# The experts' up pieces beside the selection: two halves of u in one matmul, added by GpSimd

## Chip, cores, metric

The kernel runs on one core of a Trainium2 chip. The metric is the device time of one execution in microseconds (us).

## What is computed

Two transformer blocks over 256 tokens of width 1024. The change lies in the second block's expert layer (PEER), whose core in the reference is

```python
s1 = jnp.einsum('thd,hnd->thn', qh[..., :PEER_HALF], sub_keys[:, 0])
s2 = jnp.einsum('thd,hnd->thn', qh[..., PEER_HALF:], sub_keys[:, 1])
v1, i1 = lax.top_k(s1, PEER_TOPK)
v2, i2 = lax.top_k(s2, PEER_TOPK)
cand = v1[..., :, None] + v2[..., None, :]          # per head 16 x 16
vs, ci = lax.top_k(cand, PEER_TOPK)
idx = e1 * PEER_KEYS + e2                           # from i1, i2 and ci
g = jax.nn.softmax(vs, axis=-1)
z = jnp.einsum('td,thkd->thk', xc, u_experts[idx])
a = jax.nn.gelu(z) * g
return jnp.einsum('thk,thkd->td', a, v_experts[idx])
```

There are 128 x 128 experts and 8 heads that select 16 each. The kernel does not gather: it computes z for all experts, applies Gelu, multiplies by a map of weights that is zero for experts not selected, and multiplies by all of v_experts.

## The kernel before, in words

**Numbers.** Every large product is made of float32 operands split in a high part (rounded to fp32r) and a low part (the rest), by three matmuls: high x high, high x low, low x high (`mm3`, lines 197 to 201).

**Pieces.** All weights come as one stream of pieces of 128x1024 float32 (512 KB), in the order in which they are used. A ring of four holds them: SyncE (SP) loads `raw`, ScalarE (ACT) makes `w_hi` by a Copy (line 178), VectorE (DVE) makes `w_lo = raw - w_hi` (line 180), and TensorE (PE) uses both. `next_piece` issues the split of the piece three ahead (`split(c + AHEAD)`), and then lets PE wait for its own. ACT's Copy for piece c waits until PE has used piece c - 4; SP loads a slot again when DVE has split it. The last PE instruction of a piece frees the slot (`s_used`).

**Up pieces.** Piece `tile` of the experts' up stream holds 128 experts (columns) by 1024 features. `piece_b` accumulates 8 steps of k into 256 columns (tokens) of a bank: 24 matmuls of 128x256, with `w_hi` or `w_lo` as the stationary operand and `u_hi[:, k, :]` or `u_lo[:, k, :]` as the moving one. `expert_up(q, tile)` (line 1468) uses bank 4 + q, q alternating, and ACT writes Gelu of it into `Z`. PE may start a tile when the Gelu of the tile two before it is done (`s_z`).

**Selection.** Per head, `select(h)` is a chain of small DVE instructions in 12 steps: a copy of the head's scores, maxima, index searches and replacements (steps 1 to 4, on 128 columns), a cast and the candidates' sums (step 5), the same on 256 columns (steps 6 to 8), comparisons and products of two tensors (steps 9 and 10, four each), two reductions (11 and 12). All of them read and write parts of `Z` that no up tile has reached yet.

**Order of the work.** A loop on PE, ACT and DVE runs 8 iterations, one head and 8 up tiles each. `weave(ups(), select(h), 2)` writes the order out: a tile, two steps of the selection, a tile, and so on, so that tiles 0 to 5 of an iteration are followed by two steps each on DVE and tiles 6 and 7 by none. On ACT a table of functions is loaded again at each iteration's start, once for the Copy and once for Gelu.

After the loop, 4 more tiles (`ups2`) alternate with `weigh`, the softmax of the chosen scores and six transposes of PE. In front of them `scores_read`, a small memset of `rows_a` on DVE, tells ACT that the selection no longer reads the part of `Z` that they overwrite. Then comes the stage of the remaining 60 tiles: DVE makes one-hot rows (line 1603) into `rows_a` and others, ACT weighs them (line 1619), PE multiplies them into maps of weights (line 1630), and ACT and DVE bring the maps and the tiles together (lines 1640 to 1668). Last comes the down stage, 128 pieces with matmuls of 512 columns.

GpSimd (POOL) issues DMAs in the first 785 us and nothing afterwards.

Of the kernel before, what the change touches and what calls it, by code (L numbers as in the profile page):

```python
# [7 lines left out]
F32R = mybir.dt.float32r  # L8
U32 = mybir.dt.uint32
ALU = mybir.AluOpType  # L10
ACT = mybir.ActivationFunctionType
AX = mybir.AxisListType
ENG = mybir.EngineType


P = 128
T, D = 256, 1024
NT, KD = T // P, D // P
# [26 lines left out]
RING = 4  # L45
# [44 lines left out]
def build(nc, stream, x_in, gains1, gains2, gain_cols, conv_w, w_ada, b_ada, c_cols, kept_in, rope_in, na_mask_in,  # L90
          t5_in, t5_hot, rpb_pad, sinks, sub_keys, gain_out, out):
    ctx = ExitStack()
    with ctx:
        def sb(c, name, shape, dt=F32):
            return c.enter_context(nc.sbuf_tensor(name, shape, dt))

        def sem(name):
            return ctx.enter_context(nc.semaphore(name))
# [8 lines left out]
        raw = sb(ctx, "raw", [P, RING, PIECE])  # L107
        w_hi = sb(ctx, "w_hi", [P, RING, PIECE], F32R)
        w_lo = sb(ctx, "w_lo", [P, RING, PIECE], F32R)
        u_hi = sb(ctx, "u_hi", [P, KD, T], F32R)  # L110
        u_lo = sb(ctx, "u_lo", [P, KD, T], F32R)
        a_hi = sb(ctx, "a_hi", [P, 2, T], F32R)
        a_lo = sb(ctx, "a_lo", [P, 2, T], F32R)
        kept = sb(ctx, "kept", [P, 2 * P + PT])
# [30 lines left out]
        s_t5c = sem("s_t5c")  # L145
        s_park, s_back, s_out = sem("s_park"), sem("s_back"), sem("s_out")
        s_z = sem("s_z")
        s_chain = sem("s_chain")
        s_eq = sem("s_eq")
        s_hs = sem("s_hs")  # L150
# [7 lines left out]
        AC = Line(nc.scalar, sem("s_ac"))  # L158
        VE = Line(nc.vector, sem("s_ve"))
        lines = (PE, AC, VE)  # L160
        compute = bass.OrderedEngineSet([ENG.PE, ENG.Activation, ENG.DVE])
        V, S, M, G = nc.vector, nc.scalar, nc.tensor, nc.gpsimd

        at = {"piece": 0, "quads": 0}
# [27 lines left out]
        def used(instruction):  # L192

            instruction.then_inc(s_used, 1)
            return s_used, dyn(RING) + at["piece"]
# [7 lines left out]
        def piece_b(o, rhs_hi, rhs_lo, kt=KD, parts=1, last=False, ready=None):  # L203

            s = next_piece(last)
            for part in range(parts):
                for k in range(kt):
                    if ready is not None:
                        PE.wait(*ready[k])
                    col = (part * kt + k) * P  # L210
                    i = mm3(o[part], w_hi[:, s, col:col + P], w_lo[:, s, col:col + P],
                            rhs_hi[:, k, :], rhs_lo[:, k, :], k == 0, k == kt - 1)
            return used(i)

        def piece_a(o, lhs, ks, width, first, final):
# [25 lines left out]
        def take(i):  # L241
            PE.wait(*free.get(i, ()))
# [227 lines left out]
        def weave(main, side, every=1):  # L470

            for n, _ in enumerate(main):
                for _ in range(every):
                    next(side, None)
            for _ in side:
                pass
# [987 lines left out]
        VE.wait(m)  # L1464
        CH = Line(nc.vector, s_chain)
        S.sem_inc(s_z, 2)

        def expert_up(q, tile):

            nc.tensor.wait_ge(s_z, tile + 1)  # L1470
            m = piece_b([bank[4 + q][:, 0:T]], *U)
            nc.scalar.wait_ge(*m)
            nc.scalar.activation(Z[:, bass.ds(tile * T, T)], bank[4 + q][:, 0:T],  # L1473
                                 ACT.Gelu_apprx_tanh).then_inc(s_z, 1)

        def top16(rows_of, m):

# [15 lines left out]
        def select(h):  # L1493

            m = CH.go((), V.tensor_copy, hs, scores[:, bass.ds(h, 1), :].rearrange("p a n -> p (a n)"))
            for a2 in (0, 2):
                yield from top16([(hs[:, a * PK:(a + 1) * PK], hs2[:, a * PK:(a + 1) * PK],
                                   val[:, a, :], idx[:, a, :].bitcast(U32)) for a in (a2, a2 + 1)], m)
            m = got["chain"]
            m1 = CH.go((m,), V.tensor_copy, idxf.rearrange("p t s n -> p (t s n)"),  # L1500
                       idx.rearrange("p a n -> p (a n)").bitcast(U32))
            v4 = val.rearrange("p (t s) n -> p t s n", s=2)
            for tt in range(NT):
                m = CH.go((m,), V.tensor_tensor,
                          cand[:, tt * 256:(tt + 1) * 256].rearrange("p (i j) -> p i j", j=PT),
                          v4[:, tt, 0, :].unsqueeze(2).to_broadcast([P, PT, PT]),
                          v4[:, tt, 1, :].unsqueeze(1).to_broadcast([P, PT, PT]), ALU.add)
            yield
            yield from top16([(cand[:, tt * 256:(tt + 1) * 256], cand2[:, tt * 256:(tt + 1) * 256],
                               pick[:, 0, tt * PT:(tt + 1) * PT],  # L1510
                               pick[:, 1, tt * PT:(tt + 1) * PT].bitcast(U32)) for tt in range(NT)], m)
            m = got["chain"]
            places = pick[:, 1, :].bitcast(U32)
            CH.go((m,), V.tensor_scalar, pick_hl[:, 0:32].bitcast(U32), places, 4, None,
                  ALU.logical_shift_right)
            m2 = CH.go((m,), V.tensor_scalar, pick_hl[:, 32:64].bitcast(U32), places, 15, None,
                       ALU.bitwise_and)
            CH.go((m,), V.tensor_copy, best[:, :, bass.ds(h * PT, PT)],
                  pick[:, 0, :].rearrange("p (t n) -> p t n", t=NT))
            m = CH.go((m2, m1), V.tensor_copy, pick_f, pick_hl.bitcast(U32))  # L1520
            yield

            e5 = [eq.rearrange("p (t k m) -> p t k m", t=NT, k=PT),
                  cand2.rearrange("p (t k m) -> p t k m", t=NT, k=PT)]
            jobs = [(side, tt) for side in range(2) for tt in range(NT)]
            ms = [CH.go((m,), V.tensor_tensor, e5[side][:, tt],
                        pick_f[:, 32 * side + PT * tt:32 * side + PT * (tt + 1)].unsqueeze(2).to_broadcast(
                            [P, PT, PT]),
                        iota16.unsqueeze(1).to_broadcast([P, PT, PT]), ALU.is_equal)
                  for side, tt in jobs]  # L1530
            yield
            ms = [CH.go((ms[n],), V.tensor_tensor, e5[side][:, tt], e5[side][:, tt],
                        idxf[:, tt, side, :].unsqueeze(1).to_broadcast([P, PT, PT]), ALU.mult)
                  for n, (side, tt) in enumerate(jobs)]
            yield
            for side in range(2):
                CH.go((ms[2 * side + 1],), V.tensor_reduce, rowcol[:, side, :, bass.ds(h * PT, PT)],
                      e5[side], AX.X, ALU.add)
                yield


        quads0, piece0 = at["quads"], at["piece"]
        with nc.Fori(0, PH, engines=compute) as h:
            at["quads"], at["piece"] = quads0 + h * (SEL_PIECES // RING), piece0
            CH.restart()

            def ups():
                for j in range(SEL_PIECES):
                    expert_up(j % 2, h * SEL_PIECES + j)
                    yield  # L1550
            weave(ups(), select(h), 2)
            nc.vector.wait_ge(s_chain, CH.n)
            nc.vector.sem_clear(s_chain)
# [4 lines left out]
        def weigh():  # L1558
            b4 = best.rearrange("p t (h k) -> p (t h) k", k=PT)
            m = VE.go((), V.tensor_tensor, cand[:, 0:NT * P].rearrange("p (g k) -> p g k", k=PT), b4,  # L1560
                      b4[:, :, 0:1].to_broadcast([P, NT * PH, PT]), ALU.subtract)
            m = AC.go((m,), S.activation, best.rearrange("p t n -> p (t n)"), cand[:, 0:NT * P], ACT.Exp)
            yield
            m = VE.go((m,), V.tensor_reduce, smx[:, 0, :], b4, AX.X, ALU.add)
            m = VE.go((m,), V.reciprocal, smx[:, 1, :], smx[:, 0, :])
            m = VE.go((m,), V.tensor_tensor, b4, b4, smx[:, 1, :].unsqueeze(2).to_broadcast(
                [P, NT * PH, PT]), ALU.mult)
            yield
            PE.wait(m)
            for a, src in enumerate((best, rowcol[:, 0, :, :], rowcol[:, 1, :, :])):  # L1570
                for tt in range(NT):
                    i = M.transpose(bank[a][:, tt * P:(tt + 1) * P], src[:, tt, :], ident)
            t = PE.done(i)
            yield
            for a in range(3):
                m = VE.go((t,), V.tensor_copy, sel[:, a, :], bank[a][:, 0:T])
            got["sel"] = m
            yield

        def ups2():  # L1580
            for j in range(RING):
                expert_up(j % 2, n0 + j)
                yield

        scores_read = VE.done(V.memset(rows_a[:, 0, 0, 0:1], 0.0))
        AC.wait(scores_read)
        weave(ups2(), weigh())
        AC.wait(got["sel"])
        VE.wait(got["sel"])
# [78 lines left out]
            V.tensor_tensor(zj, zj, fresh[:, q, cut:T], ALU.mult).then_inc(s_mu, 1)  # L1668

        take(6), take(7)  # L1670
        steps = PK - FIRST
        every = steps // (groups - steps)
        made = mapped = applied = 0
# [241 lines left out]
```

## Time and profile before

| what | value |
|---|---|
| median of 3 runs | 1813.37 us (1812.82 to 1814.57) |
| the profiled execution | 1814.04 us |
| its span | 1812.6 us |
| granted clock of TensorE, mean | 0.984 |
| instructions | 33242 |
| loop of the selection, by the trace | 1017 to 1205 us |
| four tiles and softmax behind it | to 1216 us |
| stage of the maps | to about 1445 us |
| down stage and the end | to 1812 us |

The span is the time from the first to the last instruction of the one profiled execution; the time of an execution is slightly longer. Busy times of engines overlap. A matmul's duration in the rows (0.28 us for 256 columns) is longer than the distance between two, since they are pipelined: the pace is read from starts or counts. The same holds for DVE and ACT to a smaller degree. "idle before" is the engine's idle time in front of the instruction, with what released it.

### The profile page before, as it was taken

The page shows a single profiled execution, that of the slowest core. Times are in us where ns is not written, and L with a number is a line of the kernel's source. Part 1 is how long each engine was busy: PE and PEld are TensorE (multiplying, and loading weights), DVE is VectorE, ACT ScalarE, POOL GpSimd, SP SyncE. Part 2 cuts the span into 40 slices and gives each one's busy share as a digit, 9 for nine tenths or more (in the row PEclk, how much of TensorE's full clock was granted, in tenths as well). Part 3 has the DMA queues.
Part 4 walks back from the last instruction along what each step waited for, and adds up shares of the span by engine and source line. Part 5 has one row for each costly group of instructions (what it writes and reads, how often), then busy time and mean ns, then how long its engine had stood idle before and what let it go on. Part 6 is the DMA issues. An engine that isn't in the chain of part 4 may idle for free.

```text
span 1812.6 us, 33242 instructions
## 1 busy us (share of the span) xinstructions
PE 1729.1 (95%) x11638; PEld 1589.1 (88%) x11638; DVE 1353.1 (75%) x2358; ACT 911.8 (50%) x1601; POOL 63.7 (4%) x116
## 2 busy tenths in 40 slices
PE   7999899999999899978979999999999999999996
PEld 6999799988999788967869999999999988888885
DVE  6986688877976678867665799997888856666665
ACT  3345444444354434444534455567777644554553
POOL 0000011000000112100000000000000000000000
PEclk9999999999999999999989999999999999999998
DMA  6555588754444699853325355554444455555554
GB/s 206 204 187 196 171 319 274 256 186 142 161 150 165 200 340 291 253 159 105 117 70 206 125 174 180 185 186 141 139 134 136 140 174 197 190 191 196 188 194 139
DMA packets 91753, 333.87 MB, mean 184 GB/s; under 512 B 11016, under 2 KB 11192, under 8 KB 91216
## 3 DMA queue, kind: packets, MB, share of 16 engines
q1 hardware_dynamic: 79776, 289.06, 48.2%
q0 software_dynamic: 10912, 39.38, 6.6%
q10 hardware_dynamic: 976, 4.19, 0.6%
q8 instruction: 62, 1.02, 0.2%
q14 instruction: 27, 0.22, 0.0%
HBM read 330.46 MB, written 6.07 MB: 186 GB/s over the span
## 4 chain that ended last, share of the span: by engine, by line
PE 78%; DVE 14%; issue 3%; ACT 3%; DMA 2%; DVEq 0%; SPq 0%; ACTq 0%
PE bank L199 24%; PE bank L200 23%; PE bank L201 23%; DVE Z L84 6%; DVE w_lo L180 4%; PE bank L1630 3%; PE bank L249 1%; DMA raw<-stream 1%; ACT w_hi L178 1%; PE bank L1234 1%; DVE yc L84 1%; PE bank L459 1%; ACT space L84 1%; DVE st L84 1%; PE bank L743 1%
## 5 line engine op out<-in xcount | busy, mean ns | idle before, releaser
L180 DVE TENSOR_TENSOR w_lo<-raw,w_hi 128x1024 fp32r<-128x1024 f32 x546 | 661.4, 1221 | 175.9 <-ACT w_hi L178 174.4
L199 PE MATMUL bank<-u_hi,w_hi 128*128 128x256 f32 x2416 | 703.4, 291 | 23.3 <-DVE w_lo L180 10.8
L178 ACT ACTIVATE w_hi<-raw 128x1024 fp32r<-128x1024 f32 x546 | 573.7, 1052 | 278.8 <-PE bank L201 202.0
L200 PE MATMUL bank<-u_lo,w_hi 128*128 128x256 f32 x2416 | 688.1, 285 | 0.0
L201 PE MATMUL bank<-u_hi,w_lo 128*128 128x256 f32 x2416 | 688.1, 285 | 0.0
L199 PEld LDWEIGHTS bank<-u_hi,w_hi 128*128 128x128 f32 x2416 | 468.3, 194 | 38.1 <-issue 12.4
L200 PEld LDWEIGHTS bank<-u_lo,w_hi 128*128 128x128 f32 x2416 | 468.3, 194 | 4.8 <-issue 2.4
L201 PEld LDWEIGHTS bank<-u_hi,w_lo 128*128 128x128 f32 x2416 | 467.6, 194 | 0.0
L199 PE MATMUL bank<-w_hi,a_hi 128*128 128x512 f32 x768 | 300.2, 391 | 3.7 <-DVE a_lo L937 1.8
L200 PE MATMUL bank<-w_lo,a_hi 128*128 128x512 f32 x768 | 299.6, 390 | 0.0
L201 PE MATMUL bank<-w_hi,a_lo 128*128 128x512 f32 x768 | 298.8, 389 | 0.0
L199 PEld LDWEIGHTS bank<-w_hi,a_hi 128*128 128x128 f32 x768 | 144.4, 188 | 33.1 <-DVE a_lo L937 2.7
L201 PEld LDWEIGHTS bank<-w_hi,a_lo 128*128 128x128 f32 x768 | 144.2, 188 | 30.4
L200 PEld LDWEIGHTS bank<-w_lo,a_hi 128*128 128x128 f32 x768 | 144.4, 188 | 27.7
L1705 ACT ACTIVATE a_hi<-Z 128x256 fp32r (+1 forms) x128 | 53.4, 418 | 174.1 <-PE bank L201 172.3
L1707 DVE TENSOR_TENSOR a_lo<-Z,a_hi 128x256 fp32r<-128x256 f32 x128 | 54.4, 425 | 85.4 <-ACT a_hi L1705 85.4
L1619 ACT ACTIVATE rows_a<-rows_a,sel 128x128 f32<-128x128 f32 x256 | 80.8, 390 | 0.0
L1603 DVE TENSOR_TENSOR rows_a<-kept,sel 128x512 f32<-128x512 f32 x64 | 44.2, 691 | 36.5 <-PE bank L1630 36.4
L926 ACT ACTIVATE qT<-bank 128x256 f32<-128x256 f32 x64 | 24.5, 382 | 85.6 <-PE bank L201 85.5
L1473 ACT ACTIVATE Z<-bank 128x256 f32 (+1 forms) x68 | 26.1, 384 | 78.9 <-PE bank L201 78.8
L961 DVE SCALAR_TENSOR_TENSOR space<-gate,c_tmp,space 128x1024 f32 x48 | 61.4, 1280 | 0.4
L935 DVE CAST a_hi<-qT 128x256 fp32r<-128x256 f32 x64 | 19.2, 300 | 48.8 <-PE bank L201 47.9
(263 smaller groups left out, 1657.2 us busy)
## 6 DMA issues: line engine op xcount, KB each, us to landing
raw<-stream SPq DMA_DIRECT2D x546, 512.0 KB, 3.3
gate<-w_ada POOLq DMA_DIRECT2D x48, 512.0 KB, 6.5
space<-b_ada POOLq DMA_DIRECT2D x6, 512.0 KB, 4.6
t_rows<-t_by_distance POOLq DMA_DIRECT2D x8, 256.0 KB, 4.5
rpb_rows<-rpb_pad POOLq DMA_DIRECT2D x8, 224.0 KB, 4.0
gains<-gains POOLq DMA_DIRECT2D x3, 512.0 KB, 5.3
bias_a<-t_rows POOLq DMA_DIRECT2D x1, 1536.0 KB, 11.0
bias_b<-rpb_rows POOLq DMA_DIRECT2D x16, 96.0 KB, 7.7
```

The lines of the kernel that those rows point to most:

```text
L84: return self.done(method(*args, **kw))
L178: nc.scalar.activation(w_hi[:, s, :], raw[:, s, :], ACT.Copy).then_inc(s_hi, 1)
L180: nc.vector.tensor_tensor(w_lo[:, s, :], raw[:, s, :], w_hi[:, s, :].bitcast(F32), ALU.subtract).then_inc(s_split, 1)
L199: M.matmul(o, lh, rh, start=start, stop=False, skip_group_check=True)
L200: M.matmul(o, lh, rl, start=False, stop=False, skip_group_check=True)
L201: return M.matmul(o, ll, rh, start=False, stop=stop, skip_group_check=True)
L961: nc.vector.scalar_tensor_tensor(total, ada_raw[:, k % ADA_RING, :], c_act[:, k:k + 1], total, ALU.mult, ALU.add).then_inc(s_ada, 1)
L1603: return V.tensor_tensor(out, iota.unsqueeze(1).to_broadcast([P, GROUP, P]), values.unsqueeze(2).to_broadcast([P, GROUP, P]), ALU.is_equal)
L1619: i = S.activation(rows_a[:, q, e, :], rows_a[:, q, e, :], ACT.Copy, scale=share[:, e:e + 1])
L1630: i = M.matmul(bank[6 + q][:, e * P:(e + 1) * P], rows_a[:, q, e, :], rows_b[q][:, e, :].bitcast(F32), start=True, stop=True, skip_group_c ...
L1705: S.activation(a_hi[:, q, :], zj, ACT.Copy).then_inc(s_ah, 1)
L1707: V.tensor_tensor(a_lo[:, q, :], zj, a_hi[:, q, :].bitcast(F32), ALU.subtract).then_inc(s_al, 1)
```

## The change

`u_hi` and `u_lo` become one buffer, `u_both`, in which for each k the 256 columns of the high part lie before the 256 of the low part. A new `piece_halves` multiplies `w_hi` by both in one matmul of 512 columns, which fills a whole bank, and adds `w_lo` times the high part to its first 256 columns: 16 matmuls for 24, over the same number of columns. The wanted sum is then first half plus second half. For the 68 tiles of the loop and of `ups2`, ACT copies the whole bank to SBUF (into `rows_a`, unused at that time), GpSimd adds the two halves into `Z`, and ACT applies Gelu in place, one tile later (`activated`). PE's wait is now for the Copy (`s_late`) of the tile two before, ACT's Copy waits for the add (`s_halves`) of the tile two before. GpSimd joins the loop. `scores_read` is a memset of `fresh` in place of `rows_a`, and GpSimd waits for it too. In front of the stage of the maps DVE waits for the last add and PE for the last Copy. The remaining 60 up tiles keep `piece_b`.

```diff
--- before.py
+++ after.py
@@ -107,8 +107,8 @@
         raw = sb(ctx, "raw", [P, RING, PIECE])
         w_hi = sb(ctx, "w_hi", [P, RING, PIECE], F32R)
         w_lo = sb(ctx, "w_lo", [P, RING, PIECE], F32R)
-        u_hi = sb(ctx, "u_hi", [P, KD, T], F32R)
-        u_lo = sb(ctx, "u_lo", [P, KD, T], F32R)
+        u_both = sb(ctx, "u_both", [P, KD, 2, T], F32R)
+        u_hi, u_lo = u_both[:, :, 0, :], u_both[:, :, 1, :]
         a_hi = sb(ctx, "a_hi", [P, 2, T], F32R)
         a_lo = sb(ctx, "a_lo", [P, 2, T], F32R)
         kept = sb(ctx, "kept", [P, 2 * P + PT])
@@ -145,6 +145,7 @@
         s_t5c = sem("s_t5c")
         s_park, s_back, s_out = sem("s_park"), sem("s_back"), sem("s_out")
         s_z = sem("s_z")
+        s_halves, s_late = sem("s_halves"), sem("s_late")
         s_chain = sem("s_chain")
         s_eq = sem("s_eq")
         s_hs = sem("s_hs")
@@ -158,7 +159,8 @@
         AC = Line(nc.scalar, sem("s_ac"))
         VE = Line(nc.vector, sem("s_ve"))
         lines = (PE, AC, VE)
-        compute = bass.OrderedEngineSet([ENG.PE, ENG.Activation, ENG.DVE])
+        compute_list = [ENG.PE, ENG.Activation, ENG.DVE]
+        compute = bass.OrderedEngineSet(compute_list)
         V, S, M, G = nc.vector, nc.scalar, nc.tensor, nc.gpsimd
         at = {"piece": 0, "quads": 0}
@@ -210,6 +212,17 @@
                     col = (part * kt + k) * P
                     i = mm3(o[part], w_hi[:, s, col:col + P], w_lo[:, s, col:col + P],
                             rhs_hi[:, k, :], rhs_lo[:, k, :], k == 0, k == kt - 1)
+            return used(i)
+        def piece_halves(b):
+            s = next_piece()
+            for k in range(KD):
+                w = slice(k * P, (k + 1) * P)
+                M.matmul(b[:, :], w_hi[:, s, w], u_both[:, k, :, :].rearrange("p a t -> p (a t)"), start=k == 0,
+                         stop=False, skip_group_check=True)
+                i = M.matmul(b[:, 0:T], w_lo[:, s, w], u_hi[:, k, :], start=False, stop=k == KD - 1,
+                             skip_group_check=True)
             return used(i)
         def piece_a(o, lhs, ks, width, first, final):
@@ -1464,14 +1477,28 @@
         VE.wait(m)
         CH = Line(nc.vector, s_chain)
         S.sem_inc(s_z, 2)
-        def expert_up(q, tile):
-            nc.tensor.wait_ge(s_z, tile + 1)
-            m = piece_b([bank[4 + q][:, 0:T]], *U)
+        S.sem_inc(s_late, 2)
+        G.sem_inc(s_halves, 2)
+        def expert_up(q, tile, gelu=None):
+            halves = rows_a[:, q, :, :].rearrange("p a n -> p (a n)")
+            zj = Z[:, bass.ds(tile * T, T)]
+            nc.tensor.wait_ge(s_late, tile + 1)
+            m = piece_halves(bank[4 + q])
             nc.scalar.wait_ge(*m)
-            nc.scalar.activation(Z[:, bass.ds(tile * T, T)], bank[4 + q][:, 0:T],
-                                 ACT.Gelu_apprx_tanh).then_inc(s_z, 1)
+            nc.scalar.wait_ge(s_halves, tile + 1)
+            nc.scalar.activation(halves, bank[4 + q][:, :], ACT.Copy).then_inc(s_late, 1)
+            G.wait_ge(s_late, tile + 3)
+            G.tensor_tensor(zj, halves[:, 0:T], halves[:, T:2 * T], ALU.add).then_inc(s_halves, 1)
+            if gelu is not None:
+                activated(gelu)
+        def activated(tile):
+            zj = Z[:, bass.ds(tile * T, T)]
+            nc.scalar.wait_ge(s_halves, tile + 3)
+            nc.scalar.activation(zj, zj, ACT.Gelu_apprx_tanh).then_inc(s_z, 1)
         def top16(rows_of, m):
@@ -1540,14 +1567,15 @@
         quads0, piece0 = at["quads"], at["piece"]
-        with nc.Fori(0, PH, engines=compute) as h:
+        with nc.Fori(0, PH, engines=bass.OrderedEngineSet([*compute_list, ENG.Pool])) as h:
             at["quads"], at["piece"] = quads0 + h * (SEL_PIECES // RING), piece0
             CH.restart()
             def ups():
                 for j in range(SEL_PIECES):
-                    expert_up(j % 2, h * SEL_PIECES + j)
+                    expert_up(j % 2, h * SEL_PIECES + j, h * SEL_PIECES + j - 1 if j else None)
                     yield
+                activated(h * SEL_PIECES + SEL_PIECES - 1)
             weave(ups(), select(h), 2)
             nc.vector.wait_ge(s_chain, CH.n)
             nc.vector.sem_clear(s_chain)
@@ -1579,11 +1607,13 @@
         def ups2():
             for j in range(RING):
-                expert_up(j % 2, n0 + j)
-                yield
-        scores_read = VE.done(V.memset(rows_a[:, 0, 0, 0:1], 0.0))
+                expert_up(j % 2, n0 + j, n0 + j - 1 if j else None)
+                yield
+            activated(n0 + RING - 1)
+        scores_read = VE.done(V.memset(fresh[:, 0, 0:1], 0.0))
         AC.wait(scores_read)
+        G.wait_ge(*scores_read)
         weave(ups2(), weigh())
         AC.wait(got["sel"])
         VE.wait(got["sel"])
@@ -1668,6 +1698,8 @@
             V.tensor_tensor(zj, zj, fresh[:, q, cut:T], ALU.mult).then_inc(s_mu, 1)
         take(6), take(7)
+        V.wait_ge(s_halves, FIRST + 2)
+        M.wait_ge(s_late, FIRST + 2)
         steps = PK - FIRST
         every = steps // (groups - steps)
         made = mapped = applied = 0
```

## Rows read from the trace of the kernel before

**Rows 1.** The page's part 1, busy time of each engine over the span
```profile
PE 1729.1 (95%) x11638; PEld 1589.1 (88%) x11638; DVE 1353.1 (75%) x2358; ACT 911.8 (50%) x1601; POOL 63.7 (4%) x116
```

**Rows 2.** Busy time by stretch: us, then each engine's busy time (instructions)
```profile
1045.00:1070.00 25.00, 25.00 (x209) 24.82 (x208) 24.86 (x84) 14.66 (x20) 0.00 (x0) 1.00 0.55 175
1070.00:1095.00 25.00, 24.98 (x209) 24.78 (x208) 24.86 (x82) 13.65 (x20) 0.00 (x0) 1.00 0.55 183
...
1215.00:1250.00 35.00, 35.00 (x299) 35.00 (x298) 28.29 (x48) 27.27 (x76) 0.00 (x0) 1.00 0.47 151
1600.00:1700.00 100.00, 100.00 (x443) 82.81 (x442) 60.43 (x75) 50.65 (x74) 0.00 (x0) 1.00 0.58 192
```

**Rows 3.** Waits from 1040 to 1200 us: us in total, times, longest
```profile
ACT Z L1473 <- PE bank L201: 65.3, 48, 1.5
...
PEld bank L199 <- DVE w_lo L180: 1.3, 6, 0.2
DVE w_lo L180 <- ACT w_hi L178: 0.9, 1, 0.9
```

**Rows 4.** Groups of instructions, shapes apart, 1019 to 1217 us
```profile
L180 DVE TENSOR_TENSOR w_lo<-raw,w_hi 128x1024 fp32r<-128x1024 f32 x67 | 80.1, 1213 | 5.6 <-ACT w_hi L178 5.6
L178 ACT ACTIVATE w_hi<-raw 128x1024 fp32r<-128x1024 f32 x68 | 71.6, 1053 | 3.0 <-DVE rows_a L1585 3.0
L1473 ACT ACTIVATE Z<-bank 128x256 f32 x64 | 24.6, 384 | 76.5 <-PE bank L201 76.4
L84 DVE TENSOR_TENSOR Z<-Z 128x256 f32<-128x256 f32 x50 | 19.0, 419 | 0.3
```

**Rows 5.** DVE in order of time: start us, us, what [idle before]
```profile
1021.95 1.23 DVE L180 TENSOR_TENSOR w_lo<-raw,w_hi 128x1024 fp32r<-128x1024 f32 x1 [1.79 <-ACT w_hi L178]
...
1042.31 1.23 DVE L180 TENSOR_TENSOR w_lo<-raw,w_hi 128x1024 fp32r<-128x1024 f32 x1 [0.89 <-ACT w_hi L178]
1043.46 0.42 DVE L84 COPY Z<-Z 128x512 f32 x1
...
1066.79 0.42 DVE L84 COPY Z<-Z 128x512 f32 x1
...
1074.19 0.19 DVE L84 CAST Z<-Z 128x64 f32<-128x64 uint32 x1
...
1077.86 0.41 DVE L84 MATCH_REPLACE8 Z<-Z 128x256 f32<-128x256 f32 x1
...
1081.69 1.42 DVE L84 TENSOR_TENSOR Z<-Z,kept 128x256 f32<-128x256 f32 x4
...
1086.70 3.49 DVE L180 TENSOR_TENSOR w_lo<-raw,w_hi 128x1024 fp32r<-128x1024 f32 x3
```

**Rows 6.** PE in order of time, the start of a tile
```profile
1062.08 0.28 PE L201 MATMUL bank<-u_hi,w_lo 128*128 128x256 f32 x1
1062.33 0.39 PE L199 MATMUL bank<-u_hi,w_hi 128*128 128x256 f32 x1
```

**Rows 7.** ACT in order of time, end of one iteration, start of the next
```profile
1062.49 0.38 ACT L1473 ACTIVATE Z<-bank 128x256 f32 x1 [1.54 <-PE bank L201]
1062.95 1.28 ACT L178 ACT_TABLE_LOAD   x1
```

**Rows 8.** A group of instructions, 900 to 1020 us
```profile
L84 ACT ACTIVATE Z<-bank 128x512 f32<-128x512 f32 x8 | 4.8, 595 | 11.7 <-PE bank L201 11.7
```

**Rows 9.** Groups of instructions of POOL, whole span
```profile
L1060 POOL DMA_DIRECT2D bias_b<-rpb_rows x16 | 10.9, 680 | 1.1 <-issue 0.9
...
L1909 POOL MEMSET const-bfloat16-1.0<- 128x1 bf16 x1 | 0.1, 102 | 0.0
```

**Rows 10.** ACT in order of time, after the loop
```profile
1215.93 0.39 ACT L1473 ACTIVATE Z<-bank 128x256 f32<-128x256 f32 x1 [2.32 <-PE bank L201]
...
1217.16 2.44 ACT L1619 ACTIVATE rows_a<-rows_a,sel 128x128 f32<-128x128 f32 x8
```

**Rows 11.** DVE in order of time, after the loop
```profile
1215.89 0.69 DVE L1603 TENSOR_TENSOR rows_a<-kept,sel 128x512 f32<-128x512 f32 x1
```

## The prediction

> **What bounds the kernel now.** I read the page first: PE is busy for 95% of the span, DVE for 75%, ACT for 50% [rows 1]. These are means over stages, and the change touches one: 68 up tiles of the experts, from 1017 to 1216 us, 64 of them in a loop of 8 iterations that also holds the selection. So I read the stretches next. In the loop the column of PE shows 24.98 of 25 us, but that of DVE shows 24.86 of 25, against 28.29 of 35 in the stage behind it [rows 2]. Two engines are full at once. PE's x209 in 25 us is a matmul every 0.1196 us, so an iteration (8 tiles of 24 matmuls) is 22.96 us of PE. DVE's iteration is read from one instruction that comes once in it, the copy of the scores: 1043.46 and 1066.79, that is 23.33 us [rows 5].
>
> Which of the two sets the pace, the waits say. From 1040 to 1200 us DVE waits once, 0.9 us at the start; PE waits for w_lo six times, 1.3 us in all [rows 3], once an iteration, as at 1062.33, where the tile starts 0.25 us behind the matmul before it and not 0.12 [rows 6]. That is the picture of a DVE that never rests and a PE that catches up with it at the end of each iteration, where two tiles come without selection work and w_lo is made three times in a row [rows 5]. PE's slack is 0.4 us of 23.3. ACT is at 14.66 of 25 us and POOL does nothing at all here [rows 2].
>
> **The change part by part.**
>
> *Matmuls.* Per k three of 256 columns become one of 512 and one of 256. A 256 goes by every 0.1196 us. The down stage has 512 alone: x443 in 100 us, 0.2257 us each [rows 2]. So a k saves 2 x 0.1196 - 0.2257 = 0.0135 us, a tile of 8 saves 0.108, 68 tiles 7.3 us of PE. The streamed columns are the same; only the weight change between the two halves is saved. In the loop PE's iteration becomes 22.1 us beside 23.33 of DVE, and DVE's instructions in it are unchanged. DVE covers it: worth 0 there. PE waits longer for w_lo, 1.2 us an iteration where it was 0.4.
>
> *ACT.* A Gelu of 256 columns out of the bank, 0.384 us [rows 4], becomes a Copy of 512 out of a bank, 0.595 us [rows 8], and a Gelu of 256 in SBUF, taken as 0.38 too. A tile costs ACT 1.05 + 0.60 + 0.38 = 2.0 us of 2.9: it fits. PE is now released by the Copy and not by the Gelu, some tenths sooner, which PE does not need. At an iteration's end ACT must wait for the last tile's add before its Gelu, and only then comes the table load of 1.28 us [rows 7] and the next w_hi; that w_hi comes some 1.5 us later behind its tile than now. The tile itself ends about 1.1 us sooner by PE's gain, and the w_hi is needed only behind two other w_lo, so I take 0. At the start DVE idled 1.79 us because w_hi stood behind the first Gelu's table load [rows 5]; now a Copy of 0.6 stands there: -1.0 us.
>
> *GpSimd.* 68 adds of 128x256 fp32 out of SBUF. No row shows one. Duration: below, DVE's pass of this shape, 0.42 us [rows 4]; above, both operands one after the other and the fixed 0.10 of POOL's smallest instruction, 2 x 0.42 + 0.10 = 0.94 [rows 4, 9]. I take 0.10 + 0.42 = 0.52, in the order of POOL's DMA instructions here [rows 9]. The add itself is hidden: its result is wanted one tile later, 2.8 us. The question is what it does to DVE. If the two engines read SBUF by ways of their own, nothing. If they share one, a DVE instruction that needs it waits for the whole add. DVE uses two ways where it reads two tensors, and plausibly in a copy: the copy moves 512 columns in 0.42 us, a two-tensor pass 256 in 0.42 [rows 4, 5]. Between 0 and a full add each time nothing in this trace decides; I take the shared way, for the two engines have no row together that excludes it, and DVE has no idle time to lose it in.
>
> By the Trainium skill, "SBUF — State Buffer", section "SBUF: two separate sides", VectorE and GpSimd share one read and write pair as an exclusive lock, held for an instruction, and a VectorE instruction with two SBUF inputs waits for a GpSimd one that reads SBUF. It speaks against this change, and no row of this trace can show it. "GPSIMD Engine Reference", section "Performance versus the Vector engine", gives 4497 ns for an add of 2048 columns; an estimate from it is 0.56 us for 256, and the sum below would be 1.0 us larger.
>
> Where the adds fall: the iteration whose tile 0 starts at 1062.33 [rows 6]. With 2.76 us a tile PE ends them at 1065.1, 1067.9, 1070.6, 1073.4, 1076.1, 1078.9, 1081.7, 1084.5 (w_lo of tiles 5, 6 and 7 end at 1074.2, 1077.8 and 1081.7 [rows 5], in time). The Copy puts an add 0.7 us behind each. At 1065.8 DVE is in the threefold w_lo, behind it stands the copy of the scores at 1066.79: the add slips in and the copy waits. 1068.6 and 1071.3 fall among maxima and index searches of one tensor: free. 1074.1 is the end of w_lo, in front of a cast and two sums at 1074.19: a hit. 1076.8 falls in w_lo, the add runs behind it beside MATCH_REPLACE8 at 1077.86: free. 1079.6: free. 1082.4 is within the eight two-tensor passes from 1081.69: a hit. 1085.2: w_lo, then reductions of one tensor: free. Three of eight: 3 x 0.52 x 8 iterations = +12.5 us, on DVE's path, which is the loop's.
>
> *Behind the loop.* In the four tiles there DVE, ACT and PE take turns through the softmax; ACT's extra 0.2 us in that chain and PE's 0.1 a tile cancel: 0. Then the one-hot rows share a buffer with the halves, so DVE waits for the last add and PE for the last Copy. Now the last Gelu starts at 1215.93 and the first one-hot runs at 1215.89, before it [rows 10, 11]. After: the Copy ends 0.7 us behind the tile, and PE, which is full here [rows 2], stands that long; Gelu, add and Gelu push w_hi and the weighing of rows, at 1217.16 now, back by some 1.3 us, of which 0.6 is not covered by PE's own delay: +1.3 us. Queued behind the waits are on DVE four one-hots and a w_lo; w_lo leads by three tiles and is not late.
>
> *Moved to strides:* u_hi and u_lo lie alternately; all writes keep runs of at least 128 columns: 0. Pool's loop has an engine of its own with nothing queued, and SP's loads follow DVE's w_lo as before: 0.
>
> **Sum.** 12.5 - 1.0 + 1.3 = +12.8 us on the profiled execution of 1814.04 us (span 1812.6), 1826.8. The median is 0.7 lower, 1813.37: 1826.
>
> **Rivals.**
> *No shared way.* Then DVE's 23.33 us stay, the loop's gain on PE vanishes into waits for w_lo, the 1.0 at the start is lost again at the first boundary, and the one-hots cost 1.3: 1814.7. For it: ACT and DVE work side by side here at unchanged durations (w_hi 1053 ns [rows 4]). Against it: nothing in the trace. 0.25.
> *PE sets the pace (faster).* If DVE's 23.33 were partly waiting for PE in disguise, all 7.3 us would count: 1813.4 - 7.3 + 1.3 = 1807.4. For it: PE is within 0.4 us of DVE. Against: PE's six waits for w_lo, and no wait of DVE. It decides below 22.1 us of DVE work an iteration, and there are 23.3. 0.10.
> *DVE goes first where both want the way.* Then adds are put off behind runs of two-tensor passes and cost about 0.4 us an iteration: 3 + 1.3 gives 1818. Part of the forecast's case, 0.15.
> *The adds become the bound.* With its waits an add above 2.76 us holds ACT's next Copy and, through it, PE. At 0.5 us more a tile that is 32 us: 1845 and more. Against: 0.94 is my upper bound. 0.05.
> *The forecast,* 0.45: 1822 with 0.42 us an add (10.1 us) to 1843 with 0.94 and a fourth hit (30 us).
>
> **Numbers.** Range 1811 to 1843: it leaves out most of the faster case and the tail of the last, and takes in both bounds of the add. 0.2% (3.6 us) is about what a measurement tells from no change. Slower: 0.45 + 0.14 + 0.05 = 0.64, same: 0.25 and the rest of a gentle lock, 0.26, faster 0.10.
>
> **What would show it.** After: the copy of the scores every 24.9 us; DVE's mean for w_lo and two-tensor passes in the loop up from 1213 and 419 ns, or gaps in front of them, those of one-tensor passes not; PEld waiting for w_lo 2.5 us and more an iteration; POOL x68 of 0.5 to 0.9 us. A period of 23.3 us means no shared way, one of 22.1 that PE was the bound. An add above 2 us, or PE waiting for ACT's Copy within the loop, would make the forecast wrong upward.

## The result, and the profile after

| kernel | median, us | ratio to before, 95% interval | DVE's iteration, us |
|---|---|---|---|
| before | 1813.87 | | 23.33 |
| the change | 1829.72 | 1.0089 (1.0078 to 1.0099) | 25.11 |

The change is slower by 15.9 us. The profiled execution's span is 1828.0 us, 15.4 above that of before.

The page's first part, then two stretches of the loop (the columns of [rows 2]), of the changed kernel:

```profile
PE 1726.9 (94%) x11094; PEld 1557.2 (85%) x11094; DVE 1368.0 (75%) x2358; ACT 947.7 (52%) x1669; POOL 128.5 (7%) x184
```

```profile
1045.00:1070.00 25.00, 22.85 (x129) 19.36 (x128) 24.67 (x73) 17.38 (x27) 7.69 (x8) 1.00 0.53 174
1070.00:1095.00 25.00, 22.86 (x128) 19.30 (x128) 24.68 (x75) 17.28 (x27) 7.54 (x8) 1.00 0.51 160
```

PE's busy time fell from 24.98 of 25 us to 22.86: the change gave it time, and the kernel makes nothing of it. DVE is as full as before (24.68), and POOL, idle before, is busy for 7.5 us. The waits in the loop, 1040 to 1200 us (answering to [rows 3]):

```profile
PEld bank L222 <- DVE w_lo L182: 17.9, 18, 1.6
PE bank L222 <- DVE w_lo L182: 12.8, 12, 1.3
ACT Z L1501 <- POOL Z L1494: 6.2, 6, 1.0
DVE w_lo L182 <- ACT w_hi L180: 1.3, 7, 0.2
```

PE's loads waited six times for w_lo before, 1.3 us; now eighteen times, 17.9 us. DVE still waits for almost nothing. So DVE is the path, as before, and its iteration is longer. DVE in order of time, one iteration of the changed kernel (answering to [rows 5]):

```profile
1042.06 0.96 DVE L84 COPY Z<-Z 128x512 f32 x1
...
1066.03 1.23 DVE L182 TENSOR_TENSOR w_lo<-raw,w_hi 128x1024 fp32r<-128x1024 f32 x1 [0.19 <-ACT w_hi L180]
1067.17 0.97 DVE L84 COPY Z<-Z 128x512 f32 x1
...
1075.23 1.30 DVE L84 TENSOR_TENSOR Z<-Z 128x256 f32<-128x256 f32 x2
...
1083.05 1.97 DVE L84 TENSOR_TENSOR Z<-Z,kept 128x256 f32<-128x256 f32 x4
1084.95 1.42 DVE L84 TENSOR_TENSOR Z<-Z 128x256 f32<-128x256 f32 x4
```

The copy of the scores, the clock of the loop, comes at 1042.06 and at 1067.17: 25.11 us, where it was 23.33. The same rows tell where the 1.78 us are. The copy takes 0.97 us and not 0.42. The two sums of candidates take 1.30 us and not 0.87. The four comparisons take 1.97 us and not 1.42; the four products behind them are at their old 1.42. Together 0.55 + 0.43 + 0.55 = 1.53 us. Each is a hold: one DVE instruction stands for a while, and its row is longer by that. GpSimd's rows show by what:

```profile
1066.73 1.12 POOL L1494 TENSOR_TENSOR Z<-rows_a 128x256 f32 x1 [3.75 <-ACT rows_a L1492]
1069.16 0.74 POOL L1494 TENSOR_TENSOR Z<-rows_a 128x256 f32 x1 [1.31 <-ACT rows_a L1492]
...
1074.62 1.62 POOL L1494 TENSOR_TENSOR Z<-rows_a 128x256 f32 x1 [1.55 <-ACT rows_a L1492]
...
1083.18 0.90 POOL L1494 TENSOR_TENSOR Z<-rows_a 128x256 f32 x1 [2.27 <-ACT rows_a L1492]
```

An add that meets nothing takes 0.74 us. The one of 1066.73 comes while DVE is in w_lo (until 1067.17), waits, and runs under the copy of the scores. That of 1074.62 comes within w_lo as well, takes 1.62 us, and the sums are late. That of 1083.18 gets in among the comparisons. So the hold goes both ways: an add waits for a DVE pass under way, and DVE's next pass of that kind waits for the add. The group means over 1040 to 1200 us tell two kinds apart:

```profile
L182 DVE TENSOR_TENSOR w_lo<-raw,w_hi 128x1024 fp32r<-128x1024 f32 x51 | 62.2, 1228 | 1.3 <-ACT w_hi L180 1.3
L84 DVE TENSOR_TENSOR Z<-Z 128x256 f32<-128x256 f32 x36 | 16.1, 486 | 0.2
...
L84 DVE MAX8 Z<-Z 128x8 f32<-128x128 f32 x56 | 13.5, 283 | 0.2
L84 DVE TENSOR_TENSOR Z<-Z,kept 128x256 f32<-128x256 f32 x24 | 11.8, 552 | 0.0
```

In the same stretch before, the passes of two tensors took 418 and 417 ns; they now average 486 and 552. Maxima, which read one tensor, stand at 283 ns, 282 before.

The rest of the iteration, 0.25 us, is mostly the wait of 0.19 at 1066.03: ACT's w_hi is late. ACT at the end of an iteration:

```profile
1063.10 0.42 ACT L1501 ACTIVATE Z<-Z  x1 [1.01 <-POOL Z L1494]
1063.64 1.28 ACT L180 ACT_TABLE_LOAD   x1
1064.94 1.06 ACT L180 ACTIVATE w_hi<-raw 128x1024 fp32r<-128x1024 f32 x1
```

Gelu of the last tile waits 1.01 us for its add, and the table load and w_hi stand behind it. Three of the six whole iterations behind the first take 25.37 us instead: in them a fourth add holds a w_lo too, 1.47 us for 1.21.

Behind the loop, DVE and then PE of the changed kernel:

```profile
1219.59 0.96 DVE L84 TENSOR_TENSOR Z<-Z 128x256 f32<-128x256 f32 x1
...
1229.58 0.69 DVE L1633 TENSOR_TENSOR rows_a<-kept,sel 128x512 f32<-128x512 f32 x1 [0.47 <-POOL Z L1494]
```

```profile
1229.07 0.36 PE L201 MATMUL bank<-u_both,w_hi 128*128 128x256 f32 x1 [1.04 <-ACT rows_a L1492]
```

The softmax's first pass is held by the first of the four adds there (0.96 us for 0.42), the first one-hot waits 0.47 us for the last add, and PE stands 1.04 us for the last Copy. From the small memset at the end of the selection to a fixed instruction of the maps' stage (ACT into `fresh`, 128x4) it is 19.27 us and was 17.31.

The sum by the two traces, from the first copy of the scores to the memset, to that instruction, and to the end: the loop 202.16 - 188.32 = +13.84 us, behind it +1.96, the down stage +1.7. The stages ahead of the loop ended 2.2 us earlier. These last two are not put down to the change: over all runs here the loop starts between 1013.9 and 1017.9 us, and the last stage takes either 363.1 to 363.2 or 364.7 to 364.8 us, whatever the kernel (the longer in the change, five_of_eight and memset_beside). What sets it is open.

### The profile page after: what moved, and what is told of

It reads as the page before. It is cut to its first block, busy times and chain, and to the rows that moved or that the text cites. A ratio compares the mean times of both kernels' runs of the same rounds, so it can differ in the third digit from the quotient of the medians.

```text
span 1828.0 us, 32595 instructions
## 1 busy us (share of the span) xinstructions
PE 1726.9 (94%) x11094; PEld 1557.2 (85%) x11094; DVE 1368.0 (75%) x2358; ACT 947.7 (52%) x1669; POOL 128.5 (7%) x184
## 4 chain that ended last, share of the span: by engine, by line
PE 77%; DVE 13%; ACT 4%; issue 3%; DMA 2%; POOL 0%; ACTq 0%; DVEq 0%; SPq 0%; POOLq 0%
PE bank L201 22%; PE bank L202 22%; PE bank L203 22%; DVE Z L84 5%; DVE w_lo L182 4%; PE bank L1660 3%; DMA raw<-stream 2%; PE bank L222 2%; ACT w_hi L180 2%; PE bank L262 1%; PE bank L1247 1%; DVE yc L84 1%; PE bank L224 1%; DVE st L84 1%; ACT space L84 1%
## 5 line engine op out<-in xcount | busy, mean ns | idle before, releaser
L201 PE MATMUL bank<-u_both,w_hi 128*128 128x256 f32 x1872 | 547.6, 293 | 20.5 <-DVE w_lo L182 8.5
L202 PE MATMUL bank<-u_both,w_hi 128*128 128x256 f32 x1872 | 533.3, 285 | 0.0
L203 PE MATMUL bank<-u_both,w_lo 128*128 128x256 f32 x1872 | 533.1, 285 | 0.0
L201 PEld LDWEIGHTS bank<-u_both,w_hi 128*128 128x128 f32 x1872 | 362.8, 194 | 34.7 <-issue 10.6
L202 PEld LDWEIGHTS bank<-u_both,w_hi 128*128 128x128 f32 x1872 | 362.6, 194 | 4.7 <-issue 2.4
L203 PEld LDWEIGHTS bank<-u_both,w_lo 128*128 128x128 f32 x1872 | 362.2, 193 | 0.0
L222 PE MATMUL bank<-u_both,w_hi 128*128 128x512 f32 x544 | 193.7, 400 | 17.4 <-DVE w_lo L182 16.1
L224 PE MATMUL bank<-u_both,w_lo 128*128 128x256 f32 x544 | 151.8, 279 | 0.0
L222 PEld LDWEIGHTS bank<-u_both,w_hi 128*128 128x128 f32 x544 | 102.0, 188 | 47.1 <-DVE w_lo L182 20.7
L224 PEld LDWEIGHTS bank<-u_both,w_lo 128*128 128x128 f32 x544 | 102.5, 188 | 0.0
L1494 POOL TENSOR_TENSOR Z<-rows_a 128x256 f32 (+1 forms) x68 | 64.7, 951 | 384.1 <-ACT rows_a L1492 384.1
```

The costliest lines, as they stand in the source:

```text
L201: M.matmul(o, lh, rh, start=start, stop=False, skip_group_check=True)
L202: M.matmul(o, lh, rl, start=False, stop=False, skip_group_check=True)
L203: return M.matmul(o, ll, rh, start=False, stop=stop, skip_group_check=True)
L222: M.matmul(b[:, :], w_hi[:, s, w], u_both[:, k, :, :].rearrange("p a t -> p (a t)"), start=k == 0, stop=False, skip_group_check=True)
L224: i = M.matmul(b[:, 0:T], w_lo[:, s, w], u_hi[:, k, :], start=False, stop=k == KD - 1, skip_group_check=True)
L1494: G.tensor_tensor(zj, halves[:, 0:T], halves[:, T:2 * T], ALU.add).then_inc(s_halves, 1)
```

## The experiments

Medians and ratios to the kernel before, each in runs beside it; the iteration is the distance of DVE's copies of the scores (in the last two rows, of the same w_lo and of the reductions).

| kernel | median, us | ratio (95%) | iteration, us |
|---|---|---|---|
| layout_only | 1812.04 | 0.9992 (0.9981 to 1.0003) | 23.32 |
| no_add | 1814.36 | 1.0001 (0.9990 to 1.0011) | 23.32 |
| add_beside | 1823.82 | 1.0052 (1.0036 to 1.0069) | 24.79 |
| loop_only | 1826.50 | 1.0064 (1.0042 to 1.0085) | 25.36 |
| dodge | 1826.26 | 1.0074 (1.0060 to 1.0089) | 24.87 or 25.11 |
| memset_beside | 1813.56 | 1.0000 (0.9991 to 1.0009) | 23.32 |
| copy_beside | 1816.67 | 1.0016 (1.0007 to 1.0025) | 23.72 |
| five_of_eight | 1823.48 | 1.0052 (1.0036 to 1.0069) | 24.30 |
| change_scores_by_act | 1822.93 | 1.0049 (1.0032 to 1.0066) | 24.67 |
| scores_by_act | 1810.67 | 0.9983 (0.9975 to 0.9992) | 23.03 |

**The layout alone.**

```diff
-        u_hi = sb(ctx, "u_hi", [P, KD, T], F32R)
-        u_lo = sb(ctx, "u_lo", [P, KD, T], F32R)
+        u_both = sb(ctx, "u_both", [P, KD, 2, T], F32R)
+        u_hi, u_lo = u_both[:, :, 0, :], u_both[:, :, 1, :]
```

> The kernel before with u_hi and u_lo as two halves of one buffer, nothing else of the change. My theory (GpSimd's adds hold DVE in the loop) gives no change: 1814 us, within 2. Rival (the strided buffer costs something in every matmul, split or transpose, all over the kernel): several us more, spread over the stages, and part of the 15.9 us of the change.

No difference that can be measured, and an iteration of 23.32 us. The layout costs nothing.

**The change without the add.**

```diff
-            nc.scalar.wait_ge(s_halves, tile + 1)
+            nc.scalar.wait_ge(s_z, tile + 1)
...
-            G.tensor_tensor(zj, halves[:, 0:T], halves[:, T:2 * T], ALU.add).then_inc(s_halves, 1)
...
-            nc.scalar.activation(zj, zj, ACT.Gelu_apprx_tanh).then_inc(s_z, 1)
+            nc.scalar.activation(zj, halves[:, 0:T], ACT.Gelu_apprx_tanh).then_inc(s_z, 1)
```

> The changed kernel without GpSimd's add: ACT's Gelu reads the first half of the copied bank alone, so the product of high part and low part of u is left out of z for 68 tiles. Matmuls, ACT's Copy and Gelu and their order stay. My theory: the DVE iteration falls from 25.1 to 23.3 us, PE waits for w_lo about 1.2 us an iteration, 1815 to 1817 us (the waits behind the loop stay). Rival (ACT's longer path, Copy then Gelu a tile later, holds w_hi and so DVE): stays at 1827 to 1830.

The iteration is DVE's 23.32 us again, though matmuls, Copy and Gelu are those of the change. Its waits in the loop:

```profile
PEld bank L222 <- DVE w_lo L182: 6.8, 7, 1.1
PE bank L222 <- DVE w_lo L182: 4.6, 7, 0.7
```

PE's loads wait 6.8 us over seven iterations, 1 us each where it was 0.2: the matmuls' gain of 0.86 us an iteration is turned into waiting. Behind the loop the stretch is 18.61 us, +1.30: the stand for the last Copy remains. The rival, ACT's longer path, falls.

**The add alone, beside the kernel before.**

```diff
+                    G.wait_ge(s_z, h * SEL_PIECES + j + 3)
+                    G.tensor_tensor(fresh[:, 0, :], rows_a_flat[:, 0:T], rows_a_flat[:, T:2 * T],
+                                    ALU.add).then_inc(s_beside, 1)
```

> The kernel before with one GpSimd add of 128x256 fp32 on spare buffers per tile of the loop, started by the tile's Gelu; matmuls, ACT and DVE as before, and nobody waits for the adds but the memset behind the loop. It leaves nothing out. My theory: DVE's two-tensor passes and its copy of the scores are held when an add runs; 2 to 4 adds of 8 hit, 0.4 to 0.6 us each, iteration 24.3 to 25.3 us, 1821 to 1829 us. Rival (the loss is in the changed PE and ACT path): 1814.

The added lines run once a tile on GpSimd; `rows_a_flat` is `rows_a[:, 0]` with its free axes in one. DVE in order of time, in this kernel:

```profile
1044.64 0.42 DVE L84 COPY Z<-Z 128x512 f32 x1
...
1069.43 0.42 DVE L84 COPY Z<-Z 128x512 f32 x1
...
1076.94 1.44 DVE L84 TENSOR_TENSOR Z<-Z 128x256 f32<-128x256 f32 x2
...
1083.35 0.62 DVE L84 TENSOR_SCALAR Z<-Z 128x32 uint32<-128x32 uint32 x2
...
1085.26 1.97 DVE L84 TENSOR_TENSOR Z<-Z,kept 128x256 f32<-128x256 f32 x4
```

Nobody waits for these adds within the loop, and DVE's iteration grows to 24.79 us: the sums 1.44 for 0.87, a shift and a bitwise and of 32 columns 0.62 for 0.27 together, the comparisons 1.97 for 1.42. That is 1.47 us, which is the growth. The adds come at other times than in the change, and hit other instructions. With no_add this shows the cause: the add costs the time without the matmuls, and the matmuls cost none without the add.

**The four tiles behind the loop as before.**

```diff
-                expert_up(j % 2, n0 + j, n0 + j - 1 if j else None)
...
+                m = piece_b([bank[4 + q][:, 0:T]], *U)
...
+                nc.scalar.activation(Z[:, bass.ds(tile * T, T)], bank[4 + q][:, 0:T],
+                                     ACT.Gelu_apprx_tanh).then_inc(s_z, 1)
...
-        V.wait_ge(s_halves, FIRST + 2)
-        M.wait_ge(s_late, FIRST + 2)
```

> The changed kernel, but the four tiles behind the loop are made as before (24 matmuls, Gelu out of the bank, no add) and the two waits in front of the maps are gone. My theory: the loop keeps its 25.1 us an iteration; behind it the pass held by an add (0.5 us), the wait for the last add and PE's stand for the last Copy go: 2 to 3 us less than the change, 1826 to 1828. Rival (all of it is the loop): 1829 to 1830.

The stretch behind the loop is back at 17.30 us, 1.97 less than in the change, and the loop keeps the loss. The loop itself is 0.7 us longer than in the change, since here the fourth hit on a w_lo comes in six iterations and not in three. The medians differ by 3.2 us, within what two ratios of this width allow.

**Adds put off.**

```diff
+        def gate(mark):
+            V.wait_ge(*mark)
+            V.sem_inc(s_gate, 1)
...
             G.wait_ge(s_late, tile + 3)
+            if after is not None:
+                G.wait_ge(s_gate, after)
```

> The changed kernel, with three of the eight adds of an iteration put off until DVE is past the instruction they held: tile 0's until the copy of the scores is done, tile 3's until the two sums are, tile 6's until the eight comparisons and products are. It leaves nothing out. My theory (an add costs only where DVE wants two tensors or its double-speed copy): the iteration falls from 25.1 to 23.4 to 24.0 us, the time to 1816 to 1822 us. Rival (an add costs DVE something wherever it runs): about as the change, 1827 to 1830.

The expectation was missed: 1826 us, not 1816 to 1822. DVE's groups over 1040 to 1200 us, then DVE and ACT in order of time:

```profile
L183 DVE TENSOR_TENSOR w_lo<-raw,w_hi 128x1024 fp32r<-128x1024 f32 x51 | 62.5, 1235 | 7.2 <-ACT w_hi L181 5.8 <-DVE Z L84 1.3
...
L84 DVE TENSOR_TENSOR Z<-Z 128x256 f32<-128x256 f32 x38 | 14.4, 418 | 0.2
...
L84 DVE TENSOR_TENSOR Z<-Z,kept 128x256 f32<-128x256 f32 x24 | 8.5, 416 | 0.0
```

```profile
1076.38 1.50 DVE L183 TENSOR_TENSOR w_lo<-raw,w_hi 128x1024 fp32r<-128x1024 f32 x1
...
1084.68 1.23 DVE L183 TENSOR_TENSOR w_lo<-raw,w_hi 128x1024 fp32r<-128x1024 f32 x1 [0.23 <-DVE Z L84]
...
1090.24 1.23 DVE L183 TENSOR_TENSOR w_lo<-raw,w_hi 128x1024 fp32r<-128x1024 f32 x1 [0.83 <-ACT w_hi L181]
```

```profile
1086.62 0.42 ACT L1508 ACTIVATE Z<-Z  x1 [1.10 <-POOL Z L1501]
...
1089.15 1.06 ACT L181 ACTIVATE w_hi<-raw 128x1024 fp32r<-128x1024 f32 x1
```

The holds that it aimed at are gone: 418 and 416 ns. What came in their place: ACT waits 1.10 us for the add put off, its table load and w_hi move back, and DVE waits 0.83 us for that w_hi; in three of the eight iterations the add of the next tile, pushed, holds a w_lo (1.50 for 1.21); and the three gates cost DVE 0.12, 0.13 and 0.30 us, read from the distances between its starts. It shows that the holds can be avoided, and not that avoiding them so pays.

**Five tiles of eight.**

```diff
+                    if j in (0, 3, 6):
+                        plain_up(j % 2, tile, tile - 1 if j else None, False)
```

> The changed kernel, but in the loop the tiles 0, 3 and 6 of each iteration, whose adds held DVE, are made as before (24 matmuls, Gelu out of the bank; GpSimd adds one column to count along). Tiles 1, 2, 4, 5 and 7 keep the matmuls of 512 and their adds. It leaves nothing out. Dodge put adds off and paid with ACT waiting for them; here nobody waits. My theory (an add costs only where it meets a two-tensor pass): iteration 23.3 to 23.9 us, 1814 to 1819 us. Rival (every add costs DVE some 0.2 us, 1.8 us over eight): 5/8 of it, iteration 24.4 us, 1823 to 1825 us.

DVE in order of time, two rows of an iteration:

```profile
1080.50 0.69 DVE L84 TENSOR_SCALAR Z<-Z 128x32 uint32<-128x32 uint32 x2
...
1090.29 1.23 DVE L183 TENSOR_TENSOR w_lo<-raw,w_hi 128x1024 fp32r<-128x1024 f32 x1 [0.47 <-ACT w_hi L181]
```

Again no pass of 256 columns is held (417 and 417 ns), but the iteration is 24.30 us, above the range of my theory and close to the rival's number. The rows tell them apart: one add holds the shift and the bitwise and of 32 columns (0.69 for 0.27), and DVE waits 0.47 us for w_hi, because ACT at the iteration's end waits 1.04 us for the last tile's add, and the Gelu and a table load of 1.28 us stand ahead of that w_hi. 0.42 + 0.47 is 0.9 of the 0.98 us. Not every add costs; the end of an iteration costs by itself. My theory was too narrow in both: an add holds more than two-tensor passes, and ACT's wait for an add costs too.

**Other instructions on GpSimd.** In both, GpSimd's add has one column in place of 256; behind it stands the memset in memset_beside and the copy in copy_beside. As above, `rows_a_flat` stands for `rows_a[:, 0]` with its free axes in one.

```diff
-                    G.tensor_tensor(fresh[:, 0, :], rows_a_flat[:, 0:T], rows_a_flat[:, T:2 * T],
-                                    ALU.add).then_inc(s_beside, 1)
+                    G.tensor_tensor(fresh[:, 1, 0:1], rows_a_flat[:, 0:1], rows_a_flat[:, T:T + 1], ALU.add)
+                    G.memset(fresh[:, 0, :], 0.0).then_inc(s_beside, 1)
+                    G.tensor_copy(fresh[:, 0, :], rows_a_flat[:, 0:T]).then_inc(s_beside, 1)
```

> As add_beside, but GpSimd writes 256 columns by a memset and reads none (an add of one column in front of it carries the waits). It leaves nothing out. If what DVE lacks is its second way of reading, held by GpSimd's reads: only the one-column add holds it, iteration 23.3 to 23.8 us, 1814 to 1817 us. If any GpSimd instruction with a tile in SBUF holds DVE: iteration 24.2 us and more, 1820 us and more.

> As add_beside, but GpSimd copies 256 columns: one tensor read, not two (an add of one column in front of it carries the waits). It leaves nothing out. If the hold lasts as long as GpSimd streams: shorter than the add's 0.55 us, 0.3 to 0.4 us each, iteration 24.2 to 24.6 us, 1819 to 1824 us. If a GpSimd that reads one tensor leaves the way to DVE: iteration 23.3 to 23.8 us, 1814 to 1817 us.

GpSimd in memset_beside, then DVE in it, then DVE in copy_beside:

```profile
1078.49 0.31 POOL L1558 MEMSET fresh<- 128x256 f32 x1
1081.21 2.29 POOL L1556 TENSOR_TENSOR fresh<-rows_a 128x1 f32<-128x1 f32 x1 [2.41 <-ACT Z L1475]
1083.44 0.31 POOL L1558 MEMSET fresh<- 128x256 f32 x1
```

```profile
1078.42 1.22 DVE L182 TENSOR_TENSOR w_lo<-raw,w_hi 128x1024 fp32r<-128x1024 f32 x1
1079.55 1.42 DVE L84 TENSOR_TENSOR Z<-Z,kept 128x256 f32<-128x256 f32 x4
...
1082.24 1.22 DVE L182 TENSOR_TENSOR w_lo<-raw,w_hi 128x1024 fp32r<-128x1024 f32 x1
```

```profile
1082.37 1.62 DVE L84 TENSOR_TENSOR Z<-Z,kept 128x256 f32<-128x256 f32 x4
1083.91 1.62 DVE L84 TENSOR_TENSOR Z<-Z 128x256 f32<-128x256 f32 x4
```

The memset costs nothing. One of them, at 1078.49, runs within a w_lo that keeps its 1.22 us and is itself at its usual 0.31: this memset, which only writes, and a DVE pass of two tensors go side by side. The add of one column in front of the memsets shows the other side of the hold: at 1081.21 it takes 2.29 us where it takes 0.19 alone, until the w_lo that ends DVE's run of two-tensor passes is over, at 1083.46. With the copy, which reads one tensor, the comparisons and the products are late by 0.20 us each, 0.40 us an iteration, as much as the iteration grew. By its time, 1816.7 us, and its iteration, 23.72, copy_beside falls in the range of the second case expected, a copy that leaves DVE alone; the rows show the first case all the same, a hold shorter than the add's, only 0.20 us and not 0.3 to 0.4, and twice an iteration. So in these runs the hold comes with reading, and it is shorter where GpSimd reads less.

**The copy of the scores on ACT.** In the kernel before and in the change:

```diff
-            m = CH.go((), V.tensor_copy, hs, scores[:, bass.ds(h, 1), :].rearrange("p a n -> p (a n)"))
+            V.wait_ge(s_hsw, 1)
...
+        def scores_out(h):
+            nc.scalar.wait_ge(s_hsr, h + 1)
+            nc.scalar.activation(hs, scores[:, bass.ds(h, 1), :].rearrange("p a n -> p (a n)"),
+                                 ACT.Copy).then_inc(s_hsw, 1)
```

> The changed kernel with the copy of a head's scores made by ACT, as in scores_by_act. It leaves nothing out. My theory: DVE is the path, so its iteration loses the copy (0.42 us) and the hold on it (0.54): 25.1 becomes 24.15 us, 7 to 8 us less than the change, 1820 to 1822 us. If the add then meets the next two-tensor pass instead, only the copy's 0.4 us go: 1824 to 1826 us. If PE, ACT or GpSimd set the pace: no change, 1828.

> The kernel before with the copy of a head's scores made by ACT in place of DVE, once an iteration, and nothing on GpSimd. It leaves nothing out. My theory (DVE sets the pace of the loop, by 0.4 us before PE): DVE's iteration is 0.45 us shorter, PE's 22.96 us become the bound, 23.0 us an iteration, 8 x 0.3 = 2.4 us less than before, 1811.3 us. Rival (PE paces the loop already): 1813.7.

DVE in order of time in change_scores_by_act:

```profile
1067.08 1.23 DVE L183 TENSOR_TENSOR w_lo<-raw,w_hi 128x1024 fp32r<-128x1024 f32 x1 [0.19 <-ACT w_hi L181]
...
1070.57 1.55 DVE L183 TENSOR_TENSOR w_lo<-raw,w_hi 128x1024 fp32r<-128x1024 f32 x1
...
1081.90 0.49 DVE L84 TENSOR_SCALAR Z<-Z 128x32 uint32<-128x32 uint32 x2
...
1091.75 1.22 DVE L183 TENSOR_TENSOR w_lo<-raw,w_hi 128x1024 fp32r<-128x1024 f32 x1 [0.18 <-ACT w_hi L181]
```

In the change the iteration falls to 24.67 us, by 0.44, no more than the copy's own time, as in the second case of the expectation. The hold of 0.55 us on the copy is gone, and others stand in its place. It is not the same add that hits: tile 0's, at 1068.30 now, falls among maxima and searches, but tile 1's, at 1070.31, holds a w_lo (1.55 for 1.21), and tile 5's holds the shift and the bitwise and (0.49 for 0.27). The median, 1822.9 us, lies between the ranges of the two cases. Of the 4.3 us between the spans of this execution and of the change's, 1.6 are the last stage, which here took the shorter of its two times.

In the kernel before, waits in the loop and the reductions of two iterations:

```profile
ACT Z L1476 <- PE bank L202: 62.9, 41, 1.5
DVE w_lo L181 <- ACT w_hi L179: 0.9, 1, 0.9
```

```profile
1061.83 1.27 DVE L84 TENSOR_REDUCE Z<-Z 128x512 f32 x2
...
1084.86 1.27 DVE L84 TENSOR_REDUCE Z<-Z 128x512 f32 x2
```

23.03 us an iteration, and PE waits for nothing any more: it is the bound, near the 22.96 us read from the counts of before. This version beats both, 1810.67 us, 0.17% below the kernel before; the gain is small, but the interval of its ratio leaves out 1.

## Why the prediction was right, and where its terms were off

The forecast was 1826 us, slower; 1829.7 was measured. Its mechanism is what the runs show.

*DVE bounds the loop.* Right. no_add removes PE's 0.108 us a tile and the time does not move; PE waits 1 us an iteration for w_lo, 1.2 foretold. scores_by_act takes 0.42 us off DVE and the loop follows to PE's bound.

*The two engines share a way to read, by which an add holds DVE's passes.* Right, and this was the open question; add_beside and no_add settle it. The Trainium skill's rule ("SBUF — State Buffer", section "SBUF: two separate sides") agrees with the trace: the pass behind an add waits, and the add waits for a pass under way; that the wait is only for a GpSimd that reads agrees with the memset at 1078.49. The prediction's guess that the copy of the scores needs the way too is borne out by its row, 0.97 us for 0.42; it reads one tensor.

*Three of eight adds hit*: the copy of the scores, the sums, the comparisons. Right, the same three instructions. *0.52 us each*: 0.55, 0.43, 0.55, mean 0.51. That the size fits is partly luck, since two errors cancel: the add takes 0.74 us alone and not 0.52, and DVE does not wait for the whole of it. The estimate from the Trainium skill ("GPSIMD Engine Reference", section "Performance versus the Vector engine"), 0.56 us, is short of the measured 0.74 too.

*-1.0 us at the loop's start.* Right in size. DVE's waits for w_hi in the first iteration were 1.79 and 0.89 us and are 0.58, 0.94 and 0.20: 0.96 less. Adds hit there as well (a cast 0.74 us for 0.19, the eight passes of the comparisons 3.8 us for 2.7), and from the first to the second copy of the scores it took 26.98 us where it was 26.20.

*ACT at the iteration's end: 0.* Missed: 0.19 us of wait for w_hi in every iteration, since the Gelu waits for the add; no_add, without the add, has no such wait. I had weighed 1.5 us of delay against a tile that ends earlier, but it does not: DVE's longer iteration moves the tiles too.

*Behind the loop +1.3 us.* no_add measured 1.30 for the stand before the maps. The change has 1.96: the hold of the softmax's first pass was not in the sum, though the same mechanism gave it.

Sum by the traces: 13.84 + 1.96 = 15.8 us, against 12.5 - 1.0 + 1.3 = 12.8. By iteration: the first +0.78, against 1.56 - 1.0 = 0.56; the six behind it +11.5 (three at 25.11, three at 25.37 us), against 6 x 1.56 = 9.4; the last, to the memset, +1.5, against 1.56. So 2.1 of the 3.0 us missed are in the six: 1.1 the wait for w_hi and 0.8 the fourth hit in three of them. The softmax's hold is 0.7, and 0.2 is in the first. The lower end of the forecast's own case, 1822 us, is not what its terms give: 1813.4 + 10.1 - 1.0 + 1.3 = 1823.8. Nothing rests on it.

## What to carry to other kernels

Read which engine sets the pace from its idle time and from who waits, not from the busiest column: PE at 99.9% had slack, DVE at 99.4% had none. Work moved to GpSimd is not free where DVE is full. Here an add of 256 columns held the next DVE pass by up to 0.57 us and a GpSimd copy by 0.20. What was held were passes of two tensors, and of one tensor the copy of the scores, the shift and bitwise and, and a cast; maxima kept their time. So count how many GpSimd instructions that read land in front of such ones. When DVE is the bound, a one-tensor copy may be better on ScalarE: that gave the kernel before 2.3 us.

## What was not expected

Putting the adds off at the right places moved the cost and did not remove it: holds of 1.5 us an iteration became 0.83 us of waiting for w_hi, 0.55 us at the gates and, in three of the eight iterations, a w_lo held by 0.29. A queue that waits for a late helper passes the delay on, here ACT with a table load of 1.28 us behind it.

Who goes first where both want the way differs. A one-column add waited 2.1 us through several ends of DVE passes (memset_beside), but an add of 256 got in after some 0.2 us, within the comparisons (0.96 and 0.90 us rows of add_beside and the change), and the same one-column add got in after 0.16 us among the products of copy_beside. So neither the size nor the kind of pass decides; what does was not tried.

DVE instructions of 32 columns and one input, a shift and a bitwise and, were held as well: 0.27 us for the two became 0.62, 0.69 and 0.49.
